# A two-layer transformer step on one core: who builds the scaled one-hots of the expert gate matrix, VectorE alone or VectorE and ScalarE

## What is computed

```
expert = e1 * N_KEYS + e2
gate = jax.nn.softmax(top_s, axis=-1)
...
u = jnp.take(peer_u, e_c, axis=0)
a = jnp.einsum("bcd,bchkd->bchk", h_c, u)
w = g_c * jax.nn.gelu(a)
vv = jnp.take(peer_v, e_c, axis=0)
return jnp.einsum("bchk,bchkd->bcd", w, vv)
```

## Time and profile before

| | us |
|---|---|
| median of 3 runs | 2714.98 |
| lowest, highest | 2705.08, 2715.26 |
| the profiled execution, its time | 2712.09 |
| its span in the profile | 2710.2 |
| first one-hot of VectorE (L1603) | 1396.66 |
| first copy of a chunk on ScalarE (L964) | 1408.29 |
| last copy of a chunk (chunk 95) | 1592.04 |
| the long loop starts on TensorE (L2113) | 1618.08 |

### The profile page before, as it was taken

One profiled execution on the slowest core, in us unless ns is written; L12 is line 12 of the kernel. 1 busy time (PEld: TensorE's weight loads), 2 busy tenths in 40 slices (PEclk: granted clock), 3 DMA queues, 4 the chain that ended last, 5 costly groups with the idle time before them and its releaser, 6 DMA issues.

```text
span 2710.2 us, 37751 instructions
## 1 busy us (share of the span) xinstructions
PE 2533.5 (93%) x13685; PEld 2154.7 (80%) x13685; DVE 1753.7 (65%) x3867; ACT 953.9 (35%) x1695; POOL 365.3 (13%) x326
## 2 busy tenths in 40 slices
PE   8998978999998977989998989999999999999998
PEld 6777777777777955784488988898988989899976
DVE  5525556553335536546899957877778787777755
ACT  4334422222223535521154544333333333333332
POOL 1001110110000000100000002332333333232300
PEclk9999988999999988999999999999999999999999
DMA  4110004663221201022024456887787877787754
GB/s 180 63 47 1 1 4 161 225 232 125 85 93 63 79 32 47 1 78 86 1 79 164 165 225 207 301 288 264 272 284 270 287 274 279 272 284 263 267 179 140
DMA packets 123077, 431.40 MB, mean 159 GB/s; under 512 B 11648, under 2 KB 36480, under 8 KB 110736
## 3 DMA queue, kind: packets, MB, share of 16 engines
q1 hardware_dynamic: 74336, 241.20, 25.8%
q0 software_dynamic: 44064, 160.98, 17.1%
q10 hardware_dynamic: 4496, 26.84, 2.5%
HBM read 399.61 MB, written 29.36 MB: 158 GB/s over the span
## 4 chain that ended last, share of the span: by engine, by line
PE 72%; DVE 16%; ACT 4%; issue 3%; DVEq 2%; DMA 1%; ACTq 1%; POOL 0%; SPq 0%
PE ps L2113 16%; PE ps L2086 14%; PE ps L1882 9%; PE ps L1836 7%; PE ps L1752 5%; PE ps L1904 4%; PE ps L2072 3%; PE ps L2146 2%; PE ps L1817 2%; DVE r L1607 1%; PE ps L2022 1%; PE ps L1789 1%; PE ps L2003 1%; DVE big L1664 1%; ACT r L677 1%
## 5 line engine op out<-in xcount | busy, mean ns | idle before, releaser
L2086 PE MATMUL ps<-hd_hi,uT_hi 128*128 128x384 f32 x1024 | 350.0, 342 | 2.3 <-ACT uT_lo L910 2.3
L2086 PE MATMUL ps<-hd_hi,uT_lo 128*128 128x384 f32 x1024 | 346.5, 338 | 0.0
L2086 PE MATMUL ps<-hd_lo,uT_hi 128*128 128x384 f32 x1024 | 346.3, 338 | 0.0
L2113 PE MATMUL ps<-v_hi,ew_hi 128*128 128x512 f32 x768 | 322.5, 420 | 9.5 <-DVE ew_lo L1580 5.3
L2113 PE MATMUL ps<-v_hi,ew_lo 128*128 128x512 f32 x768 | 305.6, 398 | 0.0
L2113 PE MATMUL ps<-v_lo,ew_hi 128*128 128x512 f32 x768 | 304.2, 396 | 0.0
L1560 DVE TENSOR_TENSOR uT_lo<-ps,uT_hi 128x512 fp32r<-128x512 f32 x204 | 140.6, 689 | 170.9 <-ACT uT_hi L883 170.6
L575 POOL DMA_INDIRECT big<-peer_u,r x128 | 144.3, 1128 | 735.8 <-DVE r L1636 437.3
L883 ACT ACTIVATE uT_hi<-ps 128x512 fp32r<-128x512 f32 x256 | 152.4, 596 | 181.8 <-PE ps L2072 181.7
L2086 PEld LDWEIGHTS ps<-hd_hi,uT_hi 128*128 128x128 f32 x1024 | 192.8, 188 | 11.3 <-ACT uT_lo L910 3.1
L2086 PEld LDWEIGHTS ps<-hd_hi,uT_lo 128*128 128x128 f32 x1024 | 192.6, 188 | 11.0
(11 more groups left out here) (338 smaller groups left out, 5241.9 us busy)
## 6 DMA issues: line engine op xcount, KB each, us to landing
big<-wst SPq DMA_DIRECT2D x70, 1024.0 KB, 4.8
r<-peer_u SPq DMA_DIRECT2D x128, 512.0 KB, 6.5
r<-peer_v SPq DMA_DIRECT2D x128, 512.0 KB, 4.8
r<-wada POOLq DMA_DIRECT2D x48, 512.0 KB, 4.6
gd<-big ACTq DMA_DIRECT2D x24, 1024.0 KB, 8.8
big<-gd SPq DMA_DIRECT2D x32, 768.0 KB, 9.7
x<-x_in SPq DMA_DIRECT2D x4, 512.0 KB, 6.8
xd<-x SPq DMA_DIRECT2D x4, 512.0 KB, 9.9
```

What stands on the lines that cost most here:

```text
L2086: mm = pe.matmul(ps[:, acc_bank(j), 0:DN], w[:, k, :], h[:, KD // 2 * half + k, :], start=(half == 0 and k == 0 and i == 0), stop=(half == ...
L2113: mm = pe.matmul(ps[:, 2 + 2 * t + half, :], w[:, P * t:P * t + P], vv[:, 512 * half:512 * half + 512], start=(i == 0 and n == 0), stop=(i ...
```

## The change

One of the four scaled one-hots of each chunk, that of its last token (k = 3), is made by ScalarE. `scaled_ones(n)` takes the distance |pick - key| for the 128 keys (`Abs` with scale -1 and the pick as pointer bias, 128 x 128), drains, and writes the positive part of gate - gate * distance (`Relu`, with `minus_gate` as pointer scale and the gate as pointer bias): at distance 0 that is the gate, at 1 or more it is 0. `minus_gate` is made once per tile. ScalarE does this three chunks ahead: chunks 0, 1, 2 before the loop, and chunk n+3 in iteration n, after the wait for chunk n and in front of the copy of chunk n. VectorE makes three scaled one-hots instead of four. TensorE waits for `scaled_ready` as well as `one_ready`. The call of `slots_evac` moves in front of the copy of its chunk.

```diff
@@ -260,6 +260,7 @@
         ranks = cut(r2, 14624, 2, SLOTS)
         wrap = rowsa[:, 0:SLOTS]
         topf = cut(r1, 11104, 2, SLOTS)
+        minus_gate, distance = rowsa[:, P:2 * P], [rowsa[:, 2 * P:3 * P], maskt]
         picks = [v.rearrange("p (a s) -> p a s", a=2) for v in (gates[:, 0, 768:1024], r1[:, 10848:11104], rowsb[:, 0:256])]
 
         gring = cut(big, 0, 2, 2 * DT, GB * HT)
@@ -344,6 +345,7 @@
             sem(n) for n in ("top3", "gate3", "idx_ready", "dots_done", "gelu_done", "u_row", "v_row"))
         y_ready, y_out, x_out, x_back = sem("y_ready"), sem("y_out"), sem("x_out"), sem("x_back")
         minus_ready, u_less = sem("minus_ready"), sem("u_less")
+        scaled_ready, keys_ready = sem("scaled_ready"), sem("keys_ready")
 
 
         pj_jobs = [(n, t) for n in range(9) for t in range(T + (n in (2, 5, 6, 7, 8)))]
@@ -926,6 +928,22 @@
                 act.wait_ge(slot_tr, t + 1)
                 act.activation(slotT[t], ps[:, 2, 0:384], ACT.Copy).then_inc(slot_ready, 1)
 
+            def scaled_ones(n):
+
+                if n >= DT * NCH:
+                    return
+                t, c = n // NCH, n % NCH
+                at = CHUNK * c + CHUNK - 1
+                if c == 0:
+                    act.drain()
+                    act.activation(minus_gate, slotT[t][:, 2 * P:3 * P], ACT.Copy, scale=-1.0)
+                act.activation(distance[n % 2], keys, ACT.Abs, scale=-1.0, bias=slotT[t][:, P + at:P + at + 1])
+                act.drain()
+                if n >= 4:
+                    act.wait_ge(g_acc, n - 3)
+                act.activation(one[n % 4][1][:, CHUNK - 1, :], distance[n % 2], ACT.Relu, scale=minus_gate[:, at:at + 1],
+                               bias=slotT[t][:, 2 * P + at:2 * P + at + 1]).then_inc(scaled_ready, 1)
+
             def half_evac(s):
 
                 if s + 1 < 2 * AHEAD:
@@ -954,6 +972,9 @@
                 if s == 14:
                     gate_exps(1)
                     gate_exps(2)
+            act.wait_ge(keys_ready, 1)
+            for n in range(3):
+                scaled_ones(n)
             for t in range(DT):
                 for c in range(NCH):
                     n = t * NCH + c
@@ -961,10 +982,11 @@
                     if at == 0:
                         stage_free(act, h)
                     act.wait_ge(g_acc, n + 1)
+                    if t < DT - 1 and c == 16:
+                        slots_evac(t + 1)
+                    scaled_ones(n + 3)
                     act.activation(stage[h % 2][:, :, at:at + CHUNK],
                                    ps[:, 5 + n % 3, :].rearrange("p (t e) -> p e t", t=CHUNK), ACT.Copy).then_inc(g_ev, 1)
-                    if t < DT - 1 and c == 16:
-                        slots_evac(t + 1)
                     if at + CHUNK == HT:
                         act.wait_ge(g_ev, n + 1)
                         for q in range(4):
@@ -1589,7 +1611,7 @@
                     if h == PH - 1 and t == 0:
                         v.drain()
                         v.wait_ge(keys_acc, 1)
-                        v.tensor_scalar(keys, ps[:, 2, 0:NKEYS], 1.0, None, ALU.subtract)
+                        v.tensor_scalar(keys, ps[:, 2, 0:NKEYS], 1.0, None, ALU.subtract).then_inc(keys_ready, 1)
                         tile_ranks(0)
                         tile_keys(0, 0)
                         tile_gates(0)
@@ -1602,7 +1624,7 @@
                         v.wait_ge(g_acc, n - 3)
                     v.tensor_tensor(one[n % 4][0], each(keys, CHUNK), over(slotT[t][:, CHUNK * c:CHUNK * c + CHUNK], NKEYS),
                                     ALU.is_equal)
-                    for k in range(CHUNK):
+                    for k in range(CHUNK - 1):
                         at = CHUNK * c + k
                         mk = v.tensor_scalar(one[n % 4][1][:, k, :], keys, slotT[t][:, P + at:P + at + 1],
                                              slotT[t][:, 2 * P + at:2 * P + at + 1], ALU.is_equal, ALU.mult)
@@ -2140,6 +2162,7 @@
                 for c in range(NCH):
                     n = t * NCH + c
                     pe.wait_ge(one_ready, n + 1)
+                    pe.wait_ge(scaled_ready, n + 1)
                     if n >= 3:
                         pe.wait_ge(g_ev, n - 2)
                     for k in range(CHUNK):
```

## The result

| | before | changed |
|---|---|---|
| median of 10 runs each, us | 2711.59 | 2725.35 |
| lowest, highest | 2705.08, 2715.26 | 2715.93, 2732.75 |
| span of the profiled execution | 2710.2 | 2726.7 |
| copy of chunk 7, start | 1429.66 | 1430.72 |
| copy of chunk 95, start | 1592.04 | 1605.96 |

The changed kernel is slower: the ratio is 1.0052, with a 95% interval of 1.0039 to 1.0064. The medians differ by 13.8 us, and so does the stage: chunk 95 is copied 1605.96 - 1592.04 = 13.9 us later, and the long loop begins 14.2 us later. (The two profiled spans differ by 16.5 us; the 2.3 us beyond that arise inside the long loop, whose code is the same.)

The account below looks back on a forecast made before the run. ScalarE was to become the stage's bound, 5.2 us above its present length; with 3 us of waits, 1 of clock and 1 of start, 10.2 us more, 2722.3 against the profiled execution, 2725 us against the median; range 2709 to 2738.

Parts of the forecast that it names:

- The price of the pair: ScalarE's `Abs`, drain and `Relu` per chunk: 0.40 + 0.07 + 0.40 = 0.87 us, bounds 0.40 and 0.97 us.
- The sum from chunk 7 to chunk 95: ScalarE's own work there: 90.3 us present, 76.6 us of pairs, 0.7 us for `minus_gate`; 167.6 us against 162.4.
- some 60: Microseconds that ScalarE idles between the copies of chunks 7 and 95, the room for the change; rows show 61.6.
- The waits that remain: In-order ScalarE still waits for TensorE at the halves: 3 us kept of the present 27.0 us.
- the clock: TensorE runs dry at five DMA issue blocks and its clock slows; ScalarE's backlog hides nearly all, 1 us in all.
- The 1.9 us for one slow patch: What TensorE's slowed clock could cost at each of five issue blocks if nothing hides it.
- The start: ScalarE's three one-hots before its first copy take 3.0 us, mostly covered by key work; 1 us taken.
- The edits at no price: Counting `keys_ready` earlier, a second semaphore on a chunk's first matmul and the moved slot copy add no time.
- The room is enough: Rival: the pairs fit into ScalarE's idle time, so faster or no change, 2701 to 2710 us; chance 0.18.
- X: ScalarE's added time per chunk for `Abs`, drain and `Relu`, taken as 0.87 us; any gain needs under about 0.78.
- ScalarE costs more, or the clock does: Rival: pair at 0.97 us, 2734 us, or slow clock unhidden behind all five issue blocks, 2733.5 us; chance 0.27.
- The signs I had named: In the stage: ScalarE's waits under 20 us, chunk 95 near 1602, VectorE waiting some 30, TensorE 15 to 25 us.

Follow-up runs that it names:

- e2: Changed kernel, but ScalarE's pair writes a scratch tile and VectorE still makes all four scaled one-hots; ratio to before 1.0074, median 2729.7 us.
- e3: Changed kernel with the 24 DMAs of the half tiles issued by GpSimd instead of ScalarE; ratio to before 0.9992, median 2706.6 us.
- e7: Changed kernel with ScalarE making the fourth scaled one-hot only in even chunks, VectorE in odd ones; ratio to before 1.0003, median 2711.6 us.
- e8: Changed kernel with a second `Relu` per chunk on ScalarE, into a scratch tile; ratio to before 1.0173, median 2760.3 us.
- e6: Changed kernel with the copy of chunk n in front of the pair for chunk n+3; ratio to before 1.0066, median 2727.1 us.
- e10: Kernel before, with GpSimd making the fourth one-hot, SyncE issuing the half-tile DMAs, ScalarE making the third in even chunks; ratio 0.9960, median 2697.2 us.
- e11: Changed kernel with ScalarE making the fourth one-hot only in even chunks and GpSimd issuing the half-tile DMAs; ratio to before 0.9977, median 2702.6 us.
- e4: Kernel before, with the 24 DMAs of the half tiles issued by GpSimd instead of ScalarE; ratio to before 0.9990, median 2708.6 us.

## Why the prediction was right, and where not

**The bound.** The forecast was 2725 us and ScalarE bound; 2725.35 us was measured, and e2, e3, e7 and e8 show that it is ScalarE. The mechanism was right. That the number fits to a third of a microsecond is luck. The order of the argument (idle time of the receiving engine in this stage, then its new sum) held. The increase was forecast at 10.2 us and is 13.8 us. The forecast stood on a median of three runs, 2715.0, and the median of before settled at 2711.6 with more: an increase 3.6 us too small was added to a start 3.4 us too high. Against the profiled execution the forecast, 2712.1 + 10.2 us, was 6 us short of 2728.5. The runs also resolve more than the 0.5% on which the chances were built: an interval of 1.0039 to 1.0064 is clear of no change.

**The price of the pair, 0.87 us:** 0.86 us. The `Abs` at 0.40 was 0.39, the drain at 0.07 was 0.07 (0.46 - 0.39), the `Relu` at 0.50 was 0.49, its step 0.40. The second pointer operand, which no row of before showed, adds about as much as the first: `Abs` with one takes 395 ns, the `Relu` with two 494 ns. By the Trainium skill (ScalarE: Activation LUTs, What ACT_TABLE_LOAD costs) that adds about 93 ns for each; the trace agrees, 99 ns, and both durations are 8 to 15 ns above its formula's 387 and 479 ns.

**The sum from chunk 7 to chunk 95, 167.6 us of ScalarE's own work.** It stands on steps, and by steps the room was 162.4 - 90.3 = 72.1 us, not the "some 60": the 61.6 us of the rows are smaller because they count each copy with its full 0.60 us. The sum doesn't use the 60, so nothing follows from this for the forecast. Two terms were mis-sized. I took 88 pairs; ScalarE makes them three chunks ahead, so 85 lie in the stretch, and 85 x 0.86 = 73.1 us stand for the 76.6. The issue blocks grew, from 17.9 to 4.2 + 3.4 + 5.0 + 3.4 + 3.3 = 19.3 us. These make 165.5 us.

**The waits that remain, "3 of the 27.0 us", and the clock, 1 us.** These two terms fell short. With them the forecast of the stretch was 171.6 us; 175.2 were measured, 9.7 us above ScalarE's own work by steps. The rows show 5.6 us of idle time in front of copies and gelus and 1.2 us in front of `Abs`; the rest is what's left when an instruction is not followed at once and its full 0.60 us count instead of 0.48. By the steps between starts, 7.1 of the 9.7 us lie in three places: 2.9 us from 1484.6 to 1489.9, 2.2 us from 1496.2 to 1499.9 and 1.9 us from 1529.0 to 1532.4. ScalarE's timeline in the second, and the granted clock there and ahead of the third (columns as above):

```profile
1496.22 0.61 ACT L885 ACTIVATE uT_hi<-ps 128x512 fp32r<-128x512 f32 x1
1497.52 0.60 ACT L912 ACTIVATE uT_lo<-ps 128x512 fp32r<-128x512 f32 x1 [0.69 <-PE ps L2116]
1499.01 0.60 ACT L885 ACTIVATE uT_hi<-ps 128x512 fp32r<-128x512 f32 x1 [0.89 <-PE ps L2094]
1499.90 0.40 ACT L940 ACTIVATE rowsa<-r,gates 128x128 f32<-128x128 f32 x1 [0.30 <-PE ps L2169]
```

```profile
1496.20:1499.90 3.70, 3.70 (x27) 3.62 (x27) 3.58 (x11) 1.83 (x4) 0.00 (x0) 1.00 0.45 142
1524.00:1528.00 4.00, 3.27 (x15) 3.01 (x15) 1.90 (x6) 3.79 (x10) 0.00 (x0) 0.50 0.88 366
```

The first two places stand behind chunks 34 and 38 (c = 2 and 6 of tile 1). There `halves_after` puts two halves in a row, to give TensorE work while VectorE does its key work. A half takes TensorE 2.77 us and ScalarE 1.0 to 1.4 us, so in the second of the two ScalarE must wait for TensorE, whatever it had to catch up. In the place shown the granted clock was 1.00 and TensorE was busy throughout; its only wait for VectorE's one-hots, 1.2 us, came at 1562.70. So it is the two halves in a row that held ScalarE there, not the missing one-hots that the prediction gave as the reason. The third place stands behind a single half, after 4 us at the lower level (0.50); in the first, both come together (0.50 from 1482 to 1484, 0.69 to 1486). An estimate from this: if two halves in a row cost 2.2 us each time, they make 4.5 us of the 7.1 and the slow clock the other 2.6, against the 1 us kept for it. No run separates them. That ScalarE's backlog hides the slow clock was right while chunks followed, and wrong where a half did. The clock fell at three issue blocks and not at five.

The 1.9 us for one slow patch were a little high: 4.59 us for 24 matmul records were held against three steps of a chunk (2.68 us), where such a group takes 2.84 us at the higher level (1419.63 in the changed kernel).

**The start, 1 us:** chunk 7 was copied 1.06 us later. Chunk 0 was 3.95 us later (1412.24 against 1408.29), and the key work covered the difference, as argued.

**The edits at no price** cost nothing that shows. ScalarE's first pair followed its last copy without a wait (1408.38 behind 1407.71), so `keys_ready` held nobody, and e6 shows no gain from another order of copy and pair.

**The rivals.** *The room is enough* was to decide at X = 0.78 us. No run lowers X alone. The nearest is e3, whose queue is shorter by the 17.9 us of issuing, as if X were 0.66 us, where I had put TensorE's floor of 148.8 us. Its stage took 158.5 us, and its runs can't be told from before. So the gain below the point is much smaller than I gave it. e7, with X at 0.43 us on average but half of VectorE's saving gone as well, comes out at the time of before. *ScalarE costs more, or the clock does* was wrong in the price and partly right in the clock. The signs I had named came true, or nearly: ScalarE's waits fell under 20 us, chunk 95 was to start near 1602 (1605.96, 4 us later), VectorE to wait some 30 us for free buffers (34.7), TensorE 15 to 25 us for ScalarE (12.7 + 4.1 + 2.7, the last for the low part at L2108, against 19.5).

## What to carry to other kernels

Before work is moved to an engine that looks idle, add up that engine's queue in the stage by steps from one start to the next, with its DMA issues in it, and compare with the length of the stage: here a move that stayed below that length was nearly free (e3, e7, e10), and above it nine tenths of each microsecond were lost (e8). Look also for places where the receiving engine must wait for another whatever its backlog, like two halves in a row. The saving on the engine that is relieved counted no further than the waits that its consumer showed for it (11.3 us of waits, 5.2 us of stage won, from 22.5 us of work). If the sum is too long, first take off the queue what another sequencer can do, or move only a part: all the pairs lost 13.8 us, all of them with the issues elsewhere neither lost nor won (e3, 0.9992), half of them with the issues elsewhere won some 6 us (e11, 0.9977).

## What was not expected

- In the changed kernel four issues of a 1 MB store each hold ScalarE 3.0 to 4.4 us, up to 5.0 us with what stands around them; the same four take GpSimd 2.1 us of its timeline in e3. In the kernel before that was nearly invisible (1.9 us of stage, e4); in the changed one taking them away gave more than the whole loss (16.7 us of stage, e3).
- GpSimd needs 1.46 us (1.34 us in e10) for a 128 x 128 fp32 one-hot with two pointer operands that takes VectorE 0.34 us, and VectorE's `tensor_scalar` grew from 342 to 357 ns beside it; it was still the better helper.
